# An f32 two-block transformer kernel on one core: the recurrent input's products dealt over the attention steps, the chunk copies of the start split over two engines, the table transposes behind the third product

## The chip, the cores and the metric

The kernel runs on 1 core of one Trainium2 chip. The metric is the device time of one execution in microseconds (us). The kernel before took 1950.97 us (median of 3 runs, 1947.81 to 1953.01).

The engines in the trace: PE is TensorE's matmul (PEld its weight load), DVE is VectorE, ACT is ScalarE, POOL is GpSimd, SP is SyncE, which here only issues DMAs. `acc` is the accumulator memory (PSUM): 4 places of 2 halves, each half 512 f32 numbers wide on 128 partitions, which is one bank.

## The reference, cut to what matters

512 tokens, with 16 meta tokens ahead in the first block, and a width of 1024. The first block has two layers: a norm, a wide projection, a pooling branch, latent attention with 8 heads, gates, and an output projection. The second block has one layer: a norm, a projection into q, k, v, the recurrent unit's input and gate, differential attention, the recurrent unit, and a mixture of experts. The change touches the start of the first block and this part of the second:

```python
q, k, v, lru_x, lru_g, gate_pre = jnp.split(proj, SPLIT_POINTS, axis=-1)
...
    def one_block(q_blk):                      # 4 query blocks of 128, 8 heads
        s = jnp.einsum('bqhcd,bkhcd->bhcqk', q_blk, k) * scale
        p = jax.nn.softmax(s, axis=-1)
        p_diff = p[:, :, 0] - lam * p[:, :, 1]
        return jnp.einsum('bhqk,bkhd->bqhd', p_diff, v)
...
xr = centred_depthwise_conv(lru_x, conv_w[l], conv_b[l])
h_fwd = rg_lru(xr, ...)                        # scan over the tokens, forwards
h_bwd = rg_lru(xr, ...)                        # and backwards
y_lru = (h_fwd + h_bwd) * jax.nn.gelu(lru_g)
```

## The kernel before, in words

All data lie with the model's width on the partitions, in 8 chunks of 128, and the tokens along the free side (528 with the meta tokens, 512 in the second block). Each product of f32 data is made from three passes, with an upper and a lower part of weights and data: upper weight by upper data, upper weight by lower data, lower weight by upper data. So a product of 1024 by 128 columns has 8 chunks x 3 = 24 passes over 512 tokens (`product3`, L1066 of the kernel before), or 48 over two halves of 264 (`product_split`, L834). The upper parts of weights are copied by ScalarE (L1449), the lower ones by VectorE (L2098), or by GpSimd for some (L2984).

The order of the work on each engine is the order of the code; engines wait for each other by semaphores. TensorE's results go to the four places of `acc` in turn: `accumulator` (L783) takes place `len(jobs) % 4` and first waits until the user of four jobs ago has been read. `drained` waits for all four.

The start: the input's four blocks of 128 tokens and the meta tokens come in as rows. For each chunk c TensorE turns four 128 x 128 blocks (L872) and the 16 meta columns (L873); VectorE copies both out (L2116, L2117); ScalarE makes the chunk's upper part (L1495), VectorE its lower part (L2110). Three weights' parts are made in between. Then follow the transposes of a vector table (`vec2`, L877) and of the rotary table (`trig`, L883), `drained`, and `first_products` (L851), which takes both its accumulators first and then goes chunk by chunk. ScalarE squares the chunks (L1444) and GpSimd adds the squares (L2898); the sum goes through `ss_h` behind the third product, and ScalarE's first evacuation (L1525, L1526) waits for it too.

The second attention has 32 items (8 heads x 4 query blocks) in 35 steps. In step s TensorE makes the scores of item s (`scores2`, L1138), an input product `lx` where `background2_at(s)` names one (8 products, one in every fourth or fifth step, the last in step 34), turns the probabilities of item s-2 (`turn2`, L1146), and multiplies the values of item s-3 (`values2`, L1155). VectorE takes the maximum (L2530) and its product with the scale (L2531), weighs the two softmaxes of item s-1 (`weigh`: L2519 to L2523), and copies `lx` out (L2537). ScalarE makes the exponentials (L1805), and copies out the turned probabilities (L1817) and the results (L1820). GpSimd makes the convolution of each `lx` chunk (L3000 to L3005) and the lower parts of `lx` weights 4 to 7. Behind the loop come the gate products `lg`, for whose weights 2 and later VectorE's lower parts stand behind the decay constants (L2544 to L2557).

## Time and profile before

| | |
|---|---|
| median of 3 runs | 1950.97 us |
| the profiled execution, its own time | 1950.18 us |
| its span, first to last instruction | 1948.2 us |
| TensorE busy | 1818.8 us, 93% |
| VectorE busy | 1176.4 us, 60% |
| ScalarE busy | 887.0 us, 46% |
| GpSimd busy | 332.0 us, 17% |
| mean granted TensorE clock | 0.978 |

A busy share is a mean over stages. The page's chain of the work that ended last has PE in 75% of the span and DVE in 15%. A number in square brackets in the timeline's rows is the idle time of the engine ahead of the row, with what ended it. The granted clock is a share of 2.4 GHz: 1.00 is that level, 0.50 the level of 1.2 GHz.

### The profile page before, as it was taken

The page shows a single profiled execution, that of the slowest core. Times are in us where ns is not written, and L with a number is a line of the kernel's source. Part 1 is how long each engine was busy: PE and PEld are TensorE (multiplying, and loading weights), DVE is VectorE, ACT ScalarE, POOL GpSimd, SP SyncE. Part 2 cuts the span into 40 slices and gives each one's busy share as a digit, 9 for nine tenths or more (in the row PEclk, how much of TensorE's full clock was granted, in tenths as well). Part 3 has the DMA queues.
Part 4 walks back from the last instruction along what each step waited for, and adds up shares of the span by engine and source line. Part 5 has one row for each costly group of instructions (what it writes and reads, how often), then busy time and mean ns, then how long its engine had stood idle before and what let it go on. Part 6 is the DMA issues. An engine that isn't in the chain of part 4 may idle for free.

```text
span 1948.2 us, 27574 instructions
## 1 busy us (share of the span) xinstructions
PE 1818.8 (93%) x11244; PEld 1542.0 (79%) x11244; DVE 1176.4 (60%) x1712; ACT 887.0 (46%) x1440; POOL 332.0 (17%) x223
## 2 busy tenths in 40 slices
PE   6999999999999999999999788899989979999993
PEld 5988788999998788999999556655568857777772
DVE  5565544554365544545774677586764456878786
ACT  3425434334334434334343454246652246777762
POOL 3332222001333222001000264510010000000001
PEclk9999999999999999999999899999999989999997
DMA  5202111223212211323222010112143258999994
GB/s 176 71 33 82 54 34 44 88 87 109 90 55 71 66 44 44 94 87 109 78 85 96 30 44 22 47 62 86 65 165 105 87 190 294 385 373 385 376 373 170
DMA packets 156103, 241.44 MB, mean 124 GB/s; under 512 B 9593, under 2 KB 101018, under 8 KB 155978
## 3 DMA queue, kind: packets, MB, share of 16 engines
q1 hardware_dynamic: 148602, 212.88, 32.4%
q0 software_dynamic: 4464, 16.25, 2.2%
q10 hardware_dynamic: 2912, 10.55, 1.3%
q8 instruction: 90, 1.47, 0.3%
q14 instruction: 35, 0.29, 0.1%
HBM read 223.41 MB, written 16.25 MB: 123 GB/s over the span
## 4 chain that ended last, share of the span: by engine, by line
PE 75%; DVE 15%; ACT 5%; issue 3%; DMA 1%; POOL 1%; SPq 0%; ACTq 0%; POOLq 0%; DVEq 0%
PE acc L834 31%; PE acc L1066 11%; PE acc L1290 9%; PE acc L1091 6%; PE acc L933 4%; PE acc L997 3%; DVE ring_split L2744 2%; PE acc L974 2%; DVE rt L2530 1%; PE acc L851 1%; PE acc L985 1%; DVE hres_split L2744 1%; PE acc L1276 1%; PE acc L1051 1%; PE acc L954 1%
## 5 line engine op out<-in xcount | busy, mean ns | idle before, releaser
L834 PE MATMUL acc<-h_split,ring_split 128*128 128x264 f32 x1088 | 309.7, 285 | 0.0
L834 PEld LDWEIGHTS acc<-h_split,ring_split 128*128 128x128 f32 x1088 | 205.7, 189 | 0.0
L834 PE MATMUL acc<-h_split,qk_split 128*128 128x264 f32 x384 | 109.7, 286 | 0.0
L834 PE MATMUL acc<-ring_split,qk_split 128*128 128x264 f32 x384 | 108.7, 283 | 0.0
L1091 PE MATMUL acc<-ring_split,h_split 128*128 128x256 f32 x384 | 107.9, 281 | 0.0
L1066 PE MATMUL acc<-h_split,ring_split 128*128 128x512 f32 x256 | 101.9, 398 | 0.0
L834 PE MATMUL acc<-h_split,krope_split 128*128 128x264 f32 x320 | 94.7, 296 | 3.9 <-ACT latent L1628 2.6
L834 PE MATMUL acc<-ring_split,krope_split 128*128 128x264 f32 x320 | 91.4, 286 | 0.0
L2098 DVE TENSOR_TENSOR ring_split<-ring,o_split 128x1024 fp32r<-128x1024 f32 (+1 forms) x32 | 44.8, 1415 | 74.8 <-ACT o_split L1449 74.8
L1290 PE MATMUL acc<-qk_split,krope_split 128*128 128x512 f32 x240 | 75.8, 397 | 8.8 <-DVE ring_split L2744 6.5
L3022 POOL DMA_INDIRECT latent<-h_rows,rows_of x16 | 18.3, 1145 | 382.9 <-PE acc L1276 230.0
L2098 DVE TENSOR_TENSOR ring_split<-ring,qk_split 128x1024 fp32r<-128x1024 f32 (+1 forms) x56 | 59.5, 1069 | 34.8 <-ACT qk_split L1449 34.6
L2898 POOL TENSOR_TENSOR latent<-latent 128x528 f32<-128x528 f32 x18 | 26.8, 1486 | 314.1 <-ACT latent L1444 313.8
L2912 POOL TENSOR_TENSOR ring_split<-ring,krope_split 128x1024 fp32r<-128x1024 f32 x20 | 48.1, 2407 | 168.7 <-ACT krope_split L1449 168.7
L997 PE MATMUL acc<-latent,v 128*64 128x128 f32 (+2 forms) x464 | 73.7, 283 | 0.9 <-ACT latent L1648 0.8
L834 PE MATMUL acc<-work_split,qk_split 128*128 128x264 f32 x256 | 72.9, 285 | 0.0
L834 PE MATMUL acc<-upad_split,ring_split 128*128 128x264 f32 x256 | 72.7, 284 | 0.0
L834 PEld LDWEIGHTS acc<-h_split,qk_split 128*128 128x128 f32 x384 | 72.3, 188 | 0.3 <-issue 0.3
L1091 PEld LDWEIGHTS acc<-ring_split,h_split 128*128 128x128 f32 x384 | 72.3, 188 | 0.0
L834 PEld LDWEIGHTS acc<-ring_split,qk_split 128*128 128x128 f32 x384 | 72.2, 188 | 0.0
L2744 DVE TENSOR_TENSOR ring_split<-ring,qk_split 128x2048 fp32r<-128x2048 f32 x24 | 54.0, 2292 | 27.5 <-ACT qk_split L1969 27.5
L1449 ACT ACTIVATE qk_split<-ring 128x1024 fp32r<-128x1024 f32 (+2 forms) x60 | 57.6, 967 | 25.7 <-PE acc L834 22.4
(572 smaller groups left out, 5806.9 us busy)
## 6 DMA issues: line engine op xcount, KB each, us to landing
ring<-in_w_in SPq DMA_DIRECT2D x64, 1024.0 KB, 5.3
ring<-in_w_expert_gate SPq DMA_DIRECT2D x13, 2048.0 KB, 9.8
ring<-in_w_expert_up SPq DMA_DIRECT2D x12, 2048.0 KB, 11.0
ring<-in_w_expert_down SPq DMA_DIRECT2D x11, 2048.0 KB, 12.1
ring<-in_w_out SPq DMA_DIRECT2D x12, 1024.0 KB, 5.7
hres<-in_w_expert_down SPq DMA_DIRECT2D x5, 2048.0 KB, 10.1
hres<-in_w_expert_up SPq DMA_DIRECT2D x4, 2048.0 KB, 11.3
y_rows<-gate ACTq DMA_DIRECT2D x16, 512.0 KB, 7.2
```

The source lines that it names most:

```text
L834: ins = nc.tensor.matmul(dst[0:rows_, half, 0:HALF], w[:, k, :], x[:, c], start=(k == 0 and i == 0), stop=(k == last and i == 2), skip_gro ...
L933: ins = nc.tensor.matmul(dst[0:nt, half, 0:width], x, w[:, c], start=(k == 0 and part == 0), stop=(k == count - 1 and part == 2), skip_gro ...
L974: ins = nc.tensor.matmul(dst[0:nt, c0:c1], qT[0:QK, hd, t0:t0 + nt], kT[0:QK, hd, c0:c1], start=True, stop=True)
L997: ins = nc.tensor.matmul(dst[r:r + VD, 0, 0:nt], v[0:nk, j, hd * VD:(hd + 1) * VD], probsT[s % 2][0:nk, j, 0:nt], start=(j == 0), stop=(j ...
L1066: ins = nc.tensor.matmul(dst[:, 0, :], w[:, k, :], x, start=(k == 0 and i == 0), stop=(k == DC - 1 and i == 2), skip_group_check=True)
L1091: ins = nc.tensor.matmul(dst[:, side, 0:WIDE], x[k][:, rows_], w, start=(k == 0 and part == 0), stop=(k == DC - 1 and part == 2), skip_gro ...
L1290: ins = nc.tensor.matmul(dst, x, w, start=start and i == 0, stop=stop and i == 2, skip_group_check=True)
L1449: nc.scalar.activation(dst, src, ACT.Copy).then_inc(act_made, 1)
L2098: made(nc.vector.tensor_tensor(dst, src, up.bitcast(F32), ALU.subtract), label)
L2744: nc.vector.tensor_tensor(granule_half(i, half, "low"), granule_half(i, half, "raw"), granule_half(i, half, "up").bitcast(F32), ALU.subtra ...
L2898: ins = nc.gpsimd.tensor_tensor(latent[:, 0, :] if c < DC - 1 else sum_sq, latent[:, 0, :], latent[:, c, :], ALU.add)
L2912: nc.gpsimd.tensor_tensor(dst, src, up.bitcast(F32), ALU.subtract).then_inc(pool_made, 1)
```

## The change

Three things.

**The input's passes are dealt over the steps.** A table says how many of the 8 x 24 = 192 passes each step makes: none in step 0, 24 in step 1, six in each of steps 2 to 25, two in each of 26 to 31, six in 32 and in 33, none in 34. `lx_passes` makes them behind the step's scores. The loop has its own places: scores alternate between places 0 and 1, a turning takes half 0 of place 2, `lx` half 1 of place 2, and values the halves of place 3 in turn. Each place is released by its own last reader. VectorE reads `lx` out ahead of `weigh`.

**The input chunks are copied by two engines.** ScalarE copies chunks 2, 5 and 7, VectorE the others. The meta tokens of all chunks are turned first into one place and copied at once.

**The tables' transposes** (`vec2`, `trig`) stand behind the third product and `ss_h` of layer 0; `drained` is gone from the start. VectorE's copies of them stand behind the reciprocal of `ss_h`.

```diff
+        LX_PASSES = 3 * DC
+        passes_at = [0, LX_PASSES] + [6] * 24 + [2] * 6 + [6, 6, 0]
+        passes_to = [sum(passes_at[:step]) for step in range(STEPS2 + 1)]
         def background2_at(step):
-            return range((step * DC) // STEPS2, ((step + 1) * DC) // STEPS2)
+            return range(passes_to[step] // LX_PASSES, passes_to[step + 1] // LX_PASSES)
...
             pe.wait_ge(x_loaded, 80)
+            dst = accumulator("meta", dve_evacuated)
             for c in range(DC):
-                dst = accumulator(("x", c), dve_evacuated)
+                ins = nc.tensor.transpose(dst[:, 0, c * META:(c + 1) * META], metain[0:META, c * P:(c + 1) * P],
+                                          ident[0:META, 0:META])
+            done(ins, "meta")
+            for c in range(DC):
+                dst = accumulator(("x", c), act_evacuated if c in X_BY_ACT else dve_evacuated)
                 for i in range(4):
-                    nc.tensor.transpose(dst[:, 0, i * P:(i + 1) * P], xin[:, i, c * P:(c + 1) * P], ident)
...
-            drained()
...
+                        if n.layer == 0:
+                            n.layer = None
+                            turn_tables()
+                            n.layer = 0
...
+            def place2_of(label, reader, slot, part):
+
+                for x in [users2[slot, part]] if (slot, part) in users2 else before2.get(slot, []):
+                    released(*x)
+                users2[slot, part] = (label, reader, n.layer)
+                n.slots[label, n.layer] = slot
+                return acc[:, slot, :, :]
+
+            def lx_passes(step):
+
+                for x in range(passes_to[step], passes_to[step + 1]):
+                    c, x = divmod(x, LX_PASSES)
+                    k, part = divmod(x, 3)
+                    label, i = ("lx", c), job_no2["lx", c]
+                    if x == 0:
+                        by = pool_made if i in LOW_BY_POOL else dve_made
+                        pe.wait_ge(by, at(by, ("wlow",) + label))
+                        lx_at.append(place2_of(label, dve_evacuated, 2, 1)[:, 1, :])
+                    w1, w0 = weight2_up(i), columns2(f"lx{c // 2}", c % 2, ring_split)
+                    w, moved = ((w1, h2_up), (w1, h2_low), (w0, h2_up))[part]
+                    ins = nc.tensor.matmul(lx_at[-1], w[:, k, :], moved[k], start=x == 0, stop=x == LX_PASSES - 1,
+                                           skip_group_check=True)
+                    if x == LX_PASSES - 1:
+                        done(ins, label)
...
-                dst = accumulator(("s2", s), act_evacuated)
+                dst = place2_of(("s2", s), act_evacuated, s % 2, 0)
...
-                dst = accumulator(("t2", s), act_evacuated)
+                dst = place2_of(("t2", s), act_evacuated, 2, 0)
...
-                dst = accumulator(("o2", s), act_evacuated)
+                dst = place2_of(("o2", s), act_evacuated, 3, s % 2)
...
-                for c in background2_at(s):
-                    product3(("lx", c), dve_evacuated, h2_up, h2_low)
+                lx_passes(s)
...
+                if c in X_BY_ACT:
+                    act.wait_ge(psum_filled, at(psum_filled, ("x", c)))
+                    nc.scalar.activation(hres[:, c, META:T], acc[:, n.slot(("x", c)), 0, :], ACT.Copy)\
+                        .then_inc(act_evacuated, 1)
...
-                if 1 <= s <= len(items2):
-                    weigh(s - 1)
                 for c in background2_at(s):
...
-                    evacuated(tt(lru_x[:, c, 1:1 + S], result2(("lx", c)), inv2, ALU.mult), ("lx", c))
+                    result2(("lx", c))
+                    evacuated(tt(lru_x[:, c, 1:1 + S], acc[:, 2, 1, :], inv2, ALU.mult), ("lx", c))
+                if 1 <= s <= len(items2):
+                    weigh(s - 1)
```

How the instructions stand now. TensorE in the second attention, from the last passes of an input product on; L1066 is a pass of the input product, L1146 a turning, L1155 the values, L1138 the scores. Before:

```order
L1066 MATMUL acc<-h_split,o_split 128x512
L1066 MATMUL acc<-ring_split,o_split 128x512
L1066 MATMUL acc<-h_split,ring_split 128x512
L1146 MATMUL acc<-const,v 128x128 x4
L1155 MATMUL acc<-upad,work 128x128 x4
L1138 MATMUL acc<-qk 128x512 x2
L1146 MATMUL acc<-const,gate 128x128 x4
L1155 MATMUL acc<-upad,work 128x128 x4
L1138 MATMUL acc<-qk 128x512 x2
L1146 MATMUL acc<-const,krope 128x128 x4
L1155 MATMUL acc<-upad,work 128x128 x4
L1138 MATMUL acc<-qk 128x512 x2
```

After, one step from turning to turning and the next (L1173 is a pass, L1195 a turning, L1204 the values, L1187 the scores):

```order
L1195 MATMUL acc<-const,gate 128x128 x4
L1187 MATMUL acc<-qk 128x512 x2
L1173 MATMUL acc<-h_split,o_split 128x512
L1173 MATMUL acc<-ring_split,o_split 128x512
L1173 MATMUL acc<-h_split,ring_split 128x512
L1173 MATMUL acc<-h_split,o_split 128x512
L1173 MATMUL acc<-ring_split,o_split 128x512
L1173 MATMUL acc<-h_split,ring_split 128x512
L1195 MATMUL acc<-const,krope 128x128 x4
L1204 MATMUL acc<-upad,work 128x128 x4
L1187 MATMUL acc<-qk 128x512 x2
```

The 24 passes that stood in one step stand as six behind each step's scores, ahead of the turning.

TensorE at the start, from the last chunk's transposes to the first passes of `first_products` (L851). Before:

```order
L872 MATMUL acc<-const,qk 128x128 x4
L873 MATMUL acc<-const,qk 128x16
L877 MATMUL acc<-const,qk 128x121
L883 MATMUL acc<-const,trig 16x32
L883 MATMUL acc<-const,trig 128x32 x4
L883 MATMUL acc<-const,trig 16x32
L883 MATMUL acc<-const,trig 128x32 x4
L851 MATMUL acc<-h_split,o_split 128x264
L851 MATMUL acc<-ring_split,o_split 128x264
L851 MATMUL acc<-h_split,ring_split 128x264
```

After: all meta columns (L879), all chunks (L885), and the first passes at once (L859).

```order
L874 MATMUL acc<-const,qk 128x44
L879 MATMUL acc<-const,qk 128x16 x8
L885 MATMUL acc<-const,qk 128x128 x32
L859 MATMUL acc<-h_split,o_split 128x264
L859 MATMUL acc<-ring_split,o_split 128x264
L859 MATMUL acc<-h_split,ring_split 128x264
```

And where the tables went: behind the third product (L842) and `ss_h` (L821), ahead of the fourth product.

```order
L842 MATMUL acc<-h_split,ring_split 128x264
L821 MATMUL acc<-gate,ones 128x264 x2
L891 MATMUL acc<-const,qk 128x121
L897 MATMUL acc<-const,trig 16x32
L897 MATMUL acc<-const,trig 128x32 x4
L897 MATMUL acc<-const,trig 16x32
L897 MATMUL acc<-const,trig 128x32 x4
L842 MATMUL acc<-h_split,o_split 128x264
L842 MATMUL acc<-ring_split,o_split 128x264
```

ScalarE at the start, behind the rotary table: L1495 makes a chunk's upper part, L1449 a weight's, L1444 the squares. Before:

```order
L1437 ACTIVATE trig<-krope,small 32x528
L1495 ACTIVATE h_split<-hres,vecs 128x528 x2
L1449 ACTIVATE o_split<-ring 128x1024
L1495 ACTIVATE h_split<-hres,vecs 128x528
L1449 ACTIVATE o_split<-ring 128x1024
L1495 ACTIVATE h_split<-hres,vecs 128x528 x3
L1449 ACTIVATE zp_split<-ring 128x1024
L1495 ACTIVATE h_split<-hres,vecs 128x528 x2
L1444 ACTIVATE latent<-hres 128x528 x8
```

After (L1546 a chunk's upper part, L1499 a weight's, L1555 the copy of a chunk out of `acc`):

```order
L1486 ACTIVATE trig<-krope,small 32x528
L1546 ACTIVATE h_split<-hres,vecs 128x528
L1499 ACTIVATE o_split<-ring 128x1024
L1546 ACTIVATE h_split<-hres,vecs 128x528
L1499 ACTIVATE o_split<-ring 128x1024
L1555 ACTIVATE hres<-acc 128x512
L1546 ACTIVATE h_split<-hres,vecs 128x528 x3
L1499 ACTIVATE zp_split<-ring 128x1024
L1555 ACTIVATE hres<-acc 128x512
L1546 ACTIVATE h_split<-hres,vecs 128x528 x2
L1555 ACTIVATE hres<-acc 128x512
L1546 ACTIVATE h_split<-hres,vecs 128x528
```

Three copies came in, and each of the three weights moved ahead by one chunk (behind chunks 0, 1 and 4 instead of 1, 2 and 5).

## Rows read from the trace of the kernel before

**Rows 1.** The page's first part: busy us, share of the span, instructions.

```profile
PE 1818.8 (93%) x11244; PEld 1542.0 (79%) x11244; DVE 1176.4 (60%) x1712; ACT 887.0 (46%) x1440; POOL 332.0 (17%) x223
```

**Rows 2.** Stretches: length, busy us of each engine, mean clock, DMA share, GB/s.

```profile
50.00:110.00 60.00, 60.00 (x490) 59.32 (x489) 37.03 (x34) 25.11 (x33) 24.57 (x11) 1.00 0.23 75
...
1079.41:1235.45 156.04, 131.49 (x705) 92.36 (x704) 108.24 (x211) 77.41 (x202) 74.91 (x53) 0.96 0.09 28
```

**Rows 3.** Timeline, TensorE, both ends of the loop: start, length, what, idle before.

```profile
1079.41 2.85 PE L1138 MATMUL acc<-qk 64*128 64x512 f32 x12
...
1089.92 1.11 PE L1146 MATMUL acc<-const,gate 128*128 128x128 f32 x4 [7.66 <-DVE gate L2523]
...
1234.40 1.05 PE L1155 MATMUL acc<-upad,work 128*128 128x128 f32 x8
```

**Rows 4.** Chain of waits, one block in the loop: start, length, what.

```profile
1114.57 5.85 PE acc L1066 x24
1120.42 0.44 PE acc L1146 x4
1120.85 0.89 PE acc L1155 x8
1121.75 1.08 PE acc L1138 x4
```

**Rows 5.** Chain of waits, VectorE's maxima, two pairs of neighbours.

```profile
1129.74 1.15 DVE rt L2530
...
1132.76 1.15 DVE rt L2530
...
1180.15 1.24 DVE rt L2530
...
1184.25 1.14 DVE rt L2530
```

**Rows 6.** Timeline of the loop: ScalarE's exponentials of step 1, VectorE's input.

```profile
1088.00 0.69 ACT L1805 ACTIVATE krope<-acc,rt 128x512 f32<-128x512 f32 x1
...
1217.32 0.69 DVE L2537 TENSOR_TENSOR latent<-acc,inv 128x512 f32<-128x512 f32 x1 [2.88 <-PE acc L1066]
```

**Rows 7.** Stretches, TensorE alone, then all engines; mean clock third from the end.

```profile
1086.00:1088.00 2.00, 0.00 (x0) 0.50 0.00 0
...
1115.00:1150.00 35.00, 31.56 (x176) 21.93 (x174) 24.77 (x49) 17.89 (x48) 19.57 (x14) 1.00 0.10 31
```

**Rows 8.** Timeline of the start, three engines.

```profile
11.16 1.12 PE L872 MATMUL acc<-const,qk 128*128 128x128 f32 x4
...
14.66 0.74 ACT L1495 ACTIVATE h_split<-hres,vecs 128x528 fp32r<-128x528 f32 x1 [0.53 <-DVE hres L2117]
...
15.31 1.04 ACT L1449 ACTIVATE o_split<-ring 128x1024 fp32r<-128x1024 f32 x1
...
15.43 0.68 DVE L2117 COPY hres<-acc 128x512 f32<-128x512 f32 x1
...
16.25 0.72 ACT L1495 ACTIVATE h_split<-hres,vecs 128x528 fp32r<-128x528 f32 x1
...
16.70 1.22 DVE L2098 TENSOR_TENSOR ring_split<-ring,o_split 128x1024 fp32r<-128x1024 f32 x1
...
22.60 1.12 PE L883 MATMUL acc<-const,trig 32*16 32x32 f32 x10 [0.90 <-DVE hres L2117]
...
28.72 0.59 PE L851 MATMUL acc<-h_split,o_split 128*128 128x264 f32 x1 [5.00 <-DVE trig L2140]
```

**Rows 9.** Chain of waits, projections of both layers.

```profile
28.72 14.02 PE acc L851 x96
...
49.45 34.81 PE acc L834 x288
...
490.15 11.64 PE acc L851 x96
```

**Rows 10.** Timeline, GpSimd's last addition of the squares.

```profile
36.66 1.34 POOL L2898 TENSOR_TENSOR gate<-latent 128x528 f32<-128x528 f32 x1
```

More of the change, by code:

```diff
@@ L786, in accumulator @@
                 if len(jobs) >= ACCS:
-                    released(*jobs[-ACCS])
-                jobs.append((label, reader, n.layer))
+                    for x in jobs[-ACCS]:
+                        released(*x)
+                jobs.append([(label, reader, n.layer)])
                 n.slots[label, n.layer] = slot
@@ L796, in drained @@
             def drained():
-                last = {x[1].name: x for x in jobs[-ACCS:]}
+                last = {x[1].name: x for users in jobs[-ACCS:] for x in users}
                 for x in last.values():
@@ L1167, in _ @@
                     values2(s - 3)
+            jobs[:] = [[x for (slot, part), x in users2.items() if slot == i] for i in range(ACCS)]
             for c in range(DC + LAG):
@@ L2120, in _ @@
+            evacuated(nc.vector.tensor_copy(hres[:, :, 0:META], src), "meta")
+            dve.wait_ge(dve_evacuated, at(dve_evacuated, "meta"))
+            for c in range(DC + 1):
+                if c < DC and c not in X_BY_ACT:
+                    result(("x", c))
+                    evacuated(nc.vector.tensor_copy(hres[:, c, META:T], acc[:, n.slot(("x", c)), 0, :]), ("x", c))
                 if c:
-                    dve.wait_ge(dve_evacuated, at(dve_evacuated, ("x", c - 1)))
+                    by = act_evacuated if c - 1 in X_BY_ACT else dve_evacuated
+                    dve.wait_ge(by, at(by, ("x", c - 1)))
@@ L2173, in _ @@
                 inverse("ss_h", inv[:, :])
+                if n.layer == 0:
+                    n.layer = None
+                    turned_tables()
+                    n.layer = 0
                 for i in range(6, DC):
```

105 lines of the change are left out of this document (56 added, 49 removed).

## The prediction

> **What bounds the kernel now.** I began with the page's busy shares: TensorE is busy 93% of the span [rows 1], so only places where it waits, or works at half clock, can give time back. Then I read the table of stretches. In the dense projections TensorE is busy in 60.00 of 60 us; in the loop of the second attention, from 1079.41 to 1235.45, it is busy 131.49 of 156.04 us, VectorE 108.24 and GpSimd 74.91, at a mean clock of 0.96 [rows 2]. So that loop waits, and no engine fills it. The timeline shows its two ends [rows 3]: the first scores at 1079.41, a wait of 7.66 us before the first turning of probabilities, and the last values ending at 1234.40 + 1.05 = 1235.45.
>
> The chain of waits shows the pattern inside [rows 4]. A whole input product of 24 passes runs 5.85 us as one block; behind it come a turning (0.43 to the next start), the values (0.90) and the next scores (1.08, with what follows 1.10), and only then VectorE's maximum. During the block VectorE and ScalarE run dry; after it TensorE waits for them, since a step without a block lasts what VectorE needs: 3.02 us from maximum to maximum, up to 4.10 with GpSimd working beside it [rows 5]. The two bounds are thus paid one after the other: about 124 us of TensorE work (below) stand in 156.
>
> The second place is the start. The first products begin at 28.72, after a wait of 5.00 us for VectorE's copies of the turned tables, while the chunks' own parts were ready long before [rows 8].
>
> **The loop, part by part.** Nothing is taken from or added to the matrix work: 192 passes, 32 scores, turnings and values. What changes is the order and the places. Before, every user took the next of four places in turn; now scores alternate between two, a turning and the input product each have a half of the third, and values alternate in the halves of the fourth. So an input product can stay open over four steps without holding up anyone, and its release falls to VectorE's one multiplication, 0.69 us [rows 6].
>
> One pass costs 5.85 / 24 = 0.24 us; a group of six 1.46, and I add 0.06 for starting each group behind another kind of product (an estimate: the block's last pass lasts longer than its share too). A six-pass step of TensorE is then 1.52 + 0.43 + 0.90 + 1.10 = 3.95 us [rows 4]. VectorE needs 3.02 free of GpSimd, at the worst 4.10 [rows 5], and 0.69 / 4 = 0.17 for its share of the input's multiplication. GpSimd's convolution is busy about half of the loop [rows 2], so VectorE's mean is near 3.5 + 0.17 = 3.7: under 3.95, by little. The order in the step leaves room: turning s is issued two steps after its scores, 7.9 + 2.6 = 10.5 us after their start, while maximum, exponentials, the next maximum and the weighing are done after some 8.5 us. That slack of 2 us covers a single step of 4.10 + 0.69.
>
> The sum, by TensorE's clock on the wall. Scores 0 and 1 begin at 1079.41 and end at 1081.4. The whole first product follows, 24 passes, until 1087.2: it fills the wait of 7.66 us. Scores 2 need the exponentials of step 0, which end at 1088.0, where those of step 1 begin [rows 6]; their VectorE inputs don't change. Scores, six passes and the first turning bring step 3 to 1091.1. Steps 3 to 25 are 23 x 3.95 = 90.9, to 1182.0. Steps 26 to 31 carry two passes each, so there VectorE sets the pace again: 6 x 3.3 = 19.8, less 1.5 of slack used up, to 1200.3. Step 32 (six passes, turning, values) 2.85 and step 33 the same, to 1206.0, the last values 0.9 more, 1206.9. For single waits on VectorE and ScalarE (an upper part of the next weights, 1.04 us [rows 8], now also lies in such a step) I add 1.5: 1208.4. The loop ends 1235.45 - 1208.4 = 27.0 us earlier. Bounds: with no such wait and no group start 30; with VectorE pacing every six-pass step at 4.27 it is 27.0 - 23 x 0.32 = 19.7.
>
> Behind the loop stand, for VectorE, two lower parts of weights and the decay constants. In both kernels they are released by the last input product, the last turning and the last values, in this order, so they move with the loop's end; the last product now ends a step earlier, which is worth nothing there, because the second lower part waits for the last turning. The loads of the later weights hang on products that now end earlier still.
>
> **The start, part by part.** The sixteen meta columns get one place and one VectorE copy: 7 small copies and 8 single turnings between chunks go, 8 small turnings stand ahead of chunk 0. From ten small ones in 1.12 us [rows 8] I take 0.9, so chunk 0 is turned at 12.05 to 13.15 instead of 11.16 to 12.3. Three of eight chunk copies (0.68 each on VectorE [rows 8]) go to ScalarE, where I take 0.65. The tables' eleven transposes leave the place where TensorE emptied all accumulators, and stand behind the third product and its sum. That is what takes the wait of 5.00 away; what is late next is chunk 5. The second accumulator of the first products is the one that chunk 5 had, and chunk 5 is now ScalarE's to copy. ScalarE's line up to it, at the pitches of before (0.65 for a chunk operation, 0.94 for a weight [rows 8]): chunk 0 in memory at 13.9, upper 0, weight 0, upper 1, weight 1 to 17.1. VectorE (a weight's lower part 1.2, the rest 0.7): lower weight 0 to 16.9, lower 1, lower weight 1 to 18.8, copy 3, lower 2, copy 4 to 20.8. ScalarE again, waiting for copy 4: upper 4, weight 2, copy 5, to 23.1. So the first products start at 23.2 instead of 28.72. They still run at the lower pace first: here 96 took 14.02, and the same 96 in the second layer, warm, 11.64 [rows 9]. 23.2 + 14.0 = 37.2; the third product 5.8 (34.81 / 6), the sum of squares 0.9 (49.45 - 42.74 - 5.80), the tables 0.9: the fourth product starts at 44.8 instead of 49.45, 4.6 us earlier. The sum of squares needs GpSimd's last addition, which ended at 38.0 [rows 10], and ScalarE's list ends about when it did, so it is in time; the fourth product now also needs the third's evacuation (43.0, and two copies of about 0.5 on ScalarE: 44.0), also in time. Bounds: 6 if ScalarE is quicker; 1.5 if chunk 5 waits longer or TensorE, fed by chunks, takes longer to reach its full pace. From there to 110 TensorE is always busy [rows 2], so the gain goes on to the end.
>
> GpSimd's and SyncE's lists keep their order; the loads move with the products that free their places.
>
> **Sum.** The profiled execution took 1950.18, its span 1948.2. 1950.18 - 27.0 - 4.6 = 1918.6. It stood 0.8 under the median of 1950.97, so I forecast 1919.
>
> **Rivals.** (A) VectorE paces the loop. For it: the step from 1180.15 to 1184.25 took 4.10 with GpSimd working [rows 5], and GpSimd's 75 us now lie in a loop of 129 us instead of 156. If all six-pass steps cost 4.27, the loop gains 19.7: 1926. Against it: most steps beside GpSimd lie well under 4.10. The Trainium skill's SBUF — State Buffer, Who interferes with whom, says that a VectorE instruction with two SBUF inputs blocks fully against a GpSimd one that reads SBUF; by that rule denser convolutions make the weighing wait for whole GpSimd instructions, which speaks for this rival; the trace agrees that such steps are longer.
>
> (B) Something behind a gain takes it back: the products behind the start wait for ScalarE's parts, or those behind the loop for VectorE's decay constants. Half of the start's gain and 4 us at the loop's end would go: 1925. TensorE is full behind the start [rows 2], which speaks against the first.
>
> (C) Slower: the clock falls inside the loop. Idle TensorE fell to 0.50 in the wait at the loop's start, and stood at 1.00 from 1115 to 1150, where its waits are short [rows 7]. If the new steps, cut into four small groups with waits between, let it fall, each us of warm work costs one more. The gain of 31.6 is used up when 31.6 / 3.95 = 8 of the 23 six-pass steps run at half clock; with 12 the time is 1919 + 47 = 1966. Against it: waits between groups get shorter, not longer. The Trainium skill's TensorE: Matmul & The Clock Gate, A second HAM failure mode: psum-queue depth-cycling, describes such an oscillation for a kernel that cycled through banks each iteration; that is this rival's mechanism, and the trace does not bear it out, with 1.00 in steps that cycled through four places.
>
> (D) The dealt passes gain nothing, because some reader still holds the input's place or the turning waits for it: 1950.97 - 4.6 = 1946. Order and places speak against it.
>
> **How the numbers follow.** Forecast 0.72, its own range 1914 to 1923; A 0.12, B 0.09, C 0.03, D 0.02, and 0.02 for slower by a cause I don't see. The range from 1912 to 1932 takes in the forecast, A and B and the bounds (loop 19.7 to 30, start 1.5 to 6, so 1950 - 36 = 1914 to 1950 - 21 = 1929), with 3 us for what no row shows. Faster by over 0.3% (6 us, about what can be told from no change) takes in the forecast, A, B and part of D: 0.94; within 0.3% 0.02; slower 0.04.
>
> **What would show it.** After: the loop's stretch about 129 us with TensorE busy over 95% of it at clock 1.00; scores to scores 3.9 to 4.0 in steps 3 to 25, and no wait of 1 us before a turning there; no wait of 7.66; the first products starting near 23.2, with the fourth near 44.8. Steps of 4.2 or more, ended by VectorE, would show A; a clock of 0.50 in the loop, C. The forecast is wrong in its main step if TensorE waits for turnings inside six-pass steps.

## The result, and the profile after

The changed kernel took 1921.35 us (median of 4 runs, 1920.62 to 1922.58) against 1949.39 of the kernel before (4 runs, 1945.62 to 1953.01): a ratio of 0.9845, 95% interval 0.983 to 0.986. The ratios given here and below are not the quotients of the two medians (here 0.9856); they differ from these by up to 0.002. The forecast was 1919.0 with a range of 1912 to 1932, so the time came out faster and inside. The profiled execution took 1922.02 with a span of 1920.2; the span of before was 1948.2, so the two traces are 28.0 us apart, and that is what has to be found in them.

The page first: busy us, share of the span, instructions, to be put beside [rows 1].

```profile
span 1920.2 us, 27569 instructions
PE 1813.5 (94%) x11244; PEld 1538.0 (80%) x11244; DVE 1179.7 (61%) x1702; ACT 887.8 (46%) x1443; POOL 331.0 (17%) x223
```

Then the stretches: after the projections the loop, from its first scores to its last values, and a part of it. Columns as in [rows 2].

```profile
1071.10:1203.31 132.21, 128.50 (x706) 88.48 (x706) 114.54 (x211) 76.43 (x202) 76.23 (x54) 1.00 0.11 35
1115.00:1150.00 35.00, 35.00 (x196) 24.43 (x195) 31.64 (x56) 19.88 (x55) 27.70 (x21) 1.00 0.10 31
```

The loop takes 132.21 us instead of 156.04 [rows 2]. TensorE's work in it is nearly the same, 128.50 busy (131.49 before, at a lower mean clock), but the idle time in it fell from 24.5 to 3.7 us, and from 1115 to 1150 there is none (before, 31.56 of 35 busy [rows 7]). VectorE's own busy time grew from 108.24 to 114.54 with the same 211 instructions.

The chain of waits of after gives the milestones at the start and behind it.

```profile
22.94 13.74 PE acc L859 x96
44.15 35.00 PE acc L842 x288
341.47 140.39 PE acc L842 x1152
1117.30 1.59 PE acc L1173 x6
1121.28 1.60 PE acc L1173 x6
1218.50 18.43 PE acc L1084 x72
1415.02 113.63 PE acc L1084 x480
```

The first products start at 22.94 (28.72 before [rows 8]), the fourth product at 44.15 (49.45 [rows 9]). Two groups of six passes in a row start 3.98 apart, where before a block of 24 ran 5.85 [rows 4]. The table follows the lead of after over before at the same piece of work. Its entries for before come from that kernel's chain of waits, except the loop's, which are [rows 3].

| piece of work | before | after | lead | gained in between |
|---|---|---|---|---|
| fourth product starts | 49.45 | 44.15 | 5.3 | start: 5.3 |
| dense products of layer 0 start (x1152) | 349.76 | 341.47 | 8.3 | first attention: 3.0 |
| loop starts | 1079.41 | 1071.10 | 8.3 | 0 |
| loop ends | 1235.45 | 1203.31 | 32.1 | loop: 23.8 |
| last long product starts (x480) | 1447.92 | 1415.02 | 32.9 | 0.8 |
| that product ends | 1559.38 | 1528.65 | 30.7 | -2.2 |
| span's end | 1948.2 | 1920.2 | 28.0 | -2.7 |

So the two changed places give 29.1, and three stretches in which nothing was changed move by 3.0, -2.2 and -2.7; with the 0.8 behind the loop that makes 28.0.

What waits are left in the loop is told by the waits by releaser, TensorE, 1071 to 1204 (waited for: us in total, times, longest).

```profile
PE acc L1195 <- ACT upad L1877: 1.7, 2, 1.2
PE acc L1195 <- DVE krope L2588: 1.1, 1, 1.1
PE acc L1187 <- ACT gate L1865: 0.9, 1, 0.9
```

These three lines hold all 3.7 us of idle time: one wait for the first exponentials, one before the turning of step 3 (the second turning of all), and two for ScalarE near the loop's end. The wait of 7.66 before the first turning [rows 3] is gone.

### The profile page after: what moved, and what is told of

It reads as the page before. It is cut to its first block, busy times and chain, and to the rows that moved or that the text cites. A ratio compares the mean times of both kernels' runs of the same rounds, so it can differ in the third digit from the quotient of the medians.

```text
span 1920.2 us, 27569 instructions
## 1 busy us (share of the span) xinstructions
PE 1813.5 (94%) x11244; PEld 1538.0 (80%) x11244; DVE 1179.7 (61%) x1702; ACT 887.8 (46%) x1443; POOL 331.0 (17%) x223
## 4 chain that ended last, share of the span: by engine, by line
PE 78%; DVE 13%; ACT 5%; issue 2%; DMA 1%; POOL 1%; SPq 0%; ACTq 0%; POOLq 0%; DVEq 0%
PE acc L842 31%; PE acc L1339 10%; PE acc L1084 8%; PE acc L1109 7%; PE acc L951 4%; PE acc L1015 3%; DVE ring_split L2810 2%; PE acc L992 2%; PE acc L1173 2%; PE acc L1187 1%; PE acc L1204 1%; PE acc L859 1%; PE acc L1003 1%; DVE hres_split L2810 1%; DVE v L2510 1%
## 5 line engine op out<-in xcount | busy, mean ns | idle before, releaser
L842 PE MATMUL acc<-h_split,ring_split 128*128 128x264 f32 x1088 | 308.4, 283 | 0.0
L842 PEld LDWEIGHTS acc<-h_split,ring_split 128*128 128x128 f32 x1088 | 204.3, 188 | 0.0
L842 PE MATMUL acc<-h_split,qk_split 128*128 128x264 f32 x384 | 109.7, 286 | 0.0
L842 PE MATMUL acc<-ring_split,qk_split 128*128 128x264 f32 x384 | 108.7, 283 | 0.0
L842 PE MATMUL acc<-h_split,krope_split 128*128 128x264 f32 x320 | 94.0, 294 | 3.8 <-ACT latent L1688 2.4
L842 PE MATMUL acc<-ring_split,krope_split 128*128 128x264 f32 x320 | 90.8, 284 | 0.0
L1084 PE MATMUL acc<-h_split,ring_split 128*128 128x512 f32 x192 | 77.4, 403 | 0.0
L842 PE MATMUL acc<-work_split,qk_split 128*128 128x264 f32 x256 | 72.9, 285 | 0.0
L842 PE MATMUL acc<-upad_split,ring_split 128*128 128x264 f32 x256 | 72.7, 284 | 0.0
L842 PEld LDWEIGHTS acc<-h_split,qk_split 128*128 128x128 f32 x384 | 72.3, 188 | 0.3 <-issue 0.3
L842 PEld LDWEIGHTS acc<-ring_split,qk_split 128*128 128x128 f32 x384 | 72.2, 188 | 0.0
L1499 ACT ACTIVATE qk_split<-ring 128x1024 fp32r<-128x1024 f32 (+2 forms) x60 | 57.7, 967 | 25.6 <-PE acc L842 24.0
## 6 DMA issues: line engine op xcount, KB each, us to landing
hres<-in_w_expert_up SPq DMA_DIRECT2D x4, 2048.0 KB, 10.8
```

Source lines behind the costliest of these rows:

```text
L842: ins = nc.tensor.matmul(dst[0:rows_, half, 0:HALF], w[:, k, :], x[:, c], start=(k == 0 and i == 0), stop=(k == last and i == 2), skip_gro ...
L1084: ins = nc.tensor.matmul(dst[:, 0, :], w[:, k, :], x, start=(k == 0 and i == 0), stop=(k == DC - 1 and i == 2), skip_group_check=True)
L1499: nc.scalar.activation(dst, src, ACT.Copy).then_inc(act_made, 1)
```

## The experiments

All times stand beside runs of the kernel before on the same chip: 1950.21 in the first four, 1952.6 in the next four, 1950.62 in the last four. "Loop" is the stretch from the first scores to the last values in each profiled execution.

### The two parts alone

e1 has the old start and the new loop; e2 the new start and the old loop, with its four places in turn.

```
e1: start as before;  passes_at = [0, 24] + [6] * 24 + [2] * 6 + [6, 6, 0], own places in the loop
e2: start as after;   24 passes where background2_at(s) names a product, places in turn
```

> The loop's part alone, on the start of before (chunks copied by VectorE, tables turned ahead of the first products, accumulators emptied). Theory: the two parts add up. The loop lasts 132 us as in the changed kernel (156 before), the first products start at 28.7 and the fourth product at 49.5, so the time is 1949.4 - 23.8 = 1925.6, give or take what the clock does elsewhere (1923 to 1929). Rival: the loop's gain needs the earlier start (the weights of the loop come in time only so): the loop over 140, time over 1933. A second rival on the 3.2 us that the first attention gained beside: if that came from the clock's phase and not from the change, its stretch from the fourth product of before (49.45) to the dense projections (349.76) keeps its 300.3 here, or takes any other value within some 3 us, though nothing before it changed.

> The start's part alone, with the loop of before. Theory: first products at 22.9, fourth product at 44.2, loop 156, time 1949.4 - 5.1 = 1944.3, and up to 3.2 less if the first attention repeats the clock of the changed kernel (297.3 us from the fourth product to the dense projections). Rival: the start's lead is lost again in the token units or the attention of the first layer, where TensorE waits for VectorE: then the dense projections start less than 3 us earlier than 349.8 and the time is 1947 or more.

e1: 1928.29 us, ratio 0.9885 (0.9866 to 0.9904); loop from 1079.65 to 1211.79, 132.1 us. e2: 1947.13, ratio 0.9995 (0.9974 to 1.0015); fourth product at 44.16, dense products at 341.55, loop from 1071.18 to 1226.23, 155.05 us. The loop's gain is there alone and whole. The start's lead is there too, 8.2 us at the dense products, but only 3.9 us of it reach the span's end (1944.3), and by the times of e2 it can't be told from nothing. So the time is the rival's (1947 or more), but not by the rival's cause, which asked for a lead under 3 us at the dense products. Set beside e1, the start does show: e1's ratio of 0.9885 and the changed kernel's 0.9845 have intervals that don't touch.

### Dealing or places

e3 keeps the own places and deals nothing. Its blocks stand in steps 1, 5, 9 to 29, those of before in steps 4, 8, 13 to 34:

```
-        passes_at = [0, LX_PASSES] + [6] * 24 + [2] * 6 + [6, 6, 0]
+        passes_at = [0] + [LX_PASSES, 0, 0, 0] * 8 + [0, 0]
```

> The changed kernel with each input product's 24 passes in one step again (steps 1, 5, 9 to 29), but with the accumulator places of the change. Theory: the dealing makes the gain, since VectorE and ScalarE run dry behind a whole block and TensorE waits for VectorE in the steps between; the loop lasts 146 to 152 us (8 blocks of 5.85, 32 steps of 3.1 to 3.5, the wait at the loop's start filled), time 1921.4 + 14 to 20 = 1935 to 1941. Rival: the own places make the gain (turnings, values and scores no longer queue behind the product's reader): the loop lasts 132 to 138 us, time 1921 to 1927.

1944.46 us, ratio 0.9975 (0.9961 to 0.9989). Its loop takes 162.0 us, 6 more than before, and its stretch (columns as in [rows 2]) and TensorE's waits in it are these.

```profile
1071.33:1233.29 161.96, 132.16 (x706) 91.86 (x706) 123.19 (x211) 77.63 (x202) 86.77 (x60) 0.97 0.10 33
```

```profile
PE acc L1195 <- ACT upad L1877: 10.7, 9, 2.6
PE acc L1195 <- DVE krope L2588: 6.5, 4, 3.1
PE acc L1195 <- DVE v L2588: 5.9, 4, 2.0
PE acc L1195 <- DVE gate L2588: 5.8, 5, 2.0
```

Both theories had the loop too short (146 to 152, and 132 to 138). All of the loop's gain needs the dealing; own places without it gain nothing. Dealing with the places in turn wasn't tried, so how much of the gain needs the own places is not shown. Why this loop is even longer than the one before isn't separated either: there are more waits for ScalarE, the blocks stand in other steps, with none in the last five, and GpSimd is busy 86.77 instead of 74.91 us, with 60 instructions instead of 53 in the loop, since the last block is done earlier.

e9 deals half as finely, twelve passes in every second step:

```
+        passes_at = [0, LX_PASSES] + [12, 0] * 12 + [2] * 6 + [6, 6, 0]
```

> The sixes of steps 2 to 25 are dealt as twelve passes in every second step and none between; everything else is the changed kernel's. Whole blocks of 24 in every fourth step took a loop of 162.0 us, sixes 132.2. Theory (a turning stands two steps behind its scores, so VectorE and ScalarE have two steps' worth of TensorE's time for it; what counts is that any two steps in a row hold twelve passes, not that each holds six): the loop takes 132 to 135 and the time is 1921 to 1924. Rival (a step without passes lasts 2.5 us on TensorE and VectorE needs 3.0 to 3.5, so each of twelve such steps waits 0.5 to 1 us or more): the loop takes 138 to 144 and the time is 1927 to 1933.

1937.64 us, ratio 0.9932 (0.991 to 0.9953); loop from 1081.95 to 1226.15, 144.2 us, TensorE busy in 130.98 of it. The rival was right on the loop, and my idea that two steps' sum is enough was wrong. Its time is above the rival's 1927 to 1933. Its seven executions run from 1930.05 to 1945.44, and in the profiled one, which took 1945.03, the loop starts 10.8 us later than in the changed kernel, by the clock in the first attention (below).

e5 deals all products evenly, which sets edges of products inside groups:

```
+        passes_at = [0, LX_PASSES] + [6, 5, 5, 5] * 8 + [0]
```

> Passes dealt evenly: 24 in step 1, then 6, 5, 5, 5 in turn to step 33, instead of sixes until step 25, twos in steps 26 to 31 and sixes in 32 and 33. In the changed kernel's trace steps 26 to 31 took 19.6 us with two passes each, while TensorE's own work in them is some 18. Theory (TensorE sets the pace of every step that has five or six passes, and the short steps at the end are where VectorE and ScalarE show): 32 steps of 5.25 passes on average cost 3.985 - 0.75 x 0.24 = 3.80 each; the loop takes 130.5 to 131.5 us instead of 132.2, the waits of 0.55 and 1.19 for ScalarE's probabilities go or shrink, and the time is 1919.5 to 1921. Rival (VectorE sets the pace nearly everywhere, at 3.9 and more): five-pass steps take as long as six-pass steps, the loop becomes 133 to 135, the time 1922 to 1924.

1928.21 us, ratio 0.9876 (0.986 to 0.9893); loop 141.5 us. Longer than either theory gave, and by something neither had. The timeline of TensorE at the first such edge, and of VectorE beside it:

```profile
1098.01 0.39 PE L1173 MATMUL acc<-h_split,ring_split 128*128 128x512 f32 x1
1099.72 0.47 PE L1173 MATMUL acc<-h_split,zp_split 128*128 128x512 f32 x1 [1.32 <-DVE latent L2601]
```

```profile
1098.89 0.69 DVE L2601 TENSOR_TENSOR latent<-acc,inv 128x512 f32<-128x512 f32 x1
```

The next product's first pass stands right behind the last one of the product before, in the same half of a place, and waits until VectorE has read it out: 7.1 us in five waits. In sixes the edges of products fall on edges of steps, and a turning, values and scores (2.4 us) lie between. Of the 9.3 us that this loop is longer, 7.1 are these waits, and 2.6 are TensorE's longer busy time (131.10 instead of 128.50) at a mean clock of 0.99.

### The order on VectorE

e4 weighs item s-1 before it reads the input product out:

```
-   for c in background2_at(s): ... read lx out ...
-   if 1 <= s <= len(items2): weigh(s - 1)
+   if 1 <= s <= len(items2): weigh(s - 1)
+   for c in background2_at(s): ... read lx out ...
```

> The changed kernel with VectorE's weighing ahead of its read of the finished input product, as before. Theory: the order is worth little, since in six-pass steps TensorE waits for neither: the read ends about 5.0 us behind the step's scores, the next product's first pass is due at 5.05; loop 132 to 133.5, time 1921 to 1923. Rival: the read in front of the weighing is what costs the waits for turnings (1.07 in step 3, and in step 26), and with the weighing first the loop gets 1 us shorter or more.

1923.32 us, ratio 0.9861 (0.9842 to 0.988); loop 135.2 us, 3.0 longer, with a wait of 1.3 for the product's place and waits of 0.9 and 0.6 before turnings. In time it can't be told from the changed kernel. The order is worth more than I expected (132 to 133.5), and the rival had its sign wrong. The changed order is the better one by 3 us in the traces; the x480 product took 111.47 here and 113.63 there, which hides most of it.

### The 3.2 us that the loop fell short

e6 moves GpSimd's lower part of a weight behind the convolution of its step; e10 deals the last product in threes.

```
e6:  weights2_lower(job_no2["lx", 4 + c]) behind the convolution of chunk c
e10: passes_at = [0, LX_PASSES] + [6] * 24 + [3] * 8 + [0]
```

> GpSimd makes its four lower weight parts of the input product behind the convolution of the same step instead of ahead of it. Theory (the first turning wait of 1.07 us in the loop comes from a VectorE instruction of 128x2 that took 1.56 us beside GpSimd's 2.35 us lower part): that instruction takes 0.17 again or another one is stretched by less, the turning of step 3 starts without a wait, the loop takes 131.0 to 131.4 instead of 132.2, the time is 1920.0 to 1920.6. Rival (GpSimd's work stretches VectorE wherever it lies, as the convolution is no kinder than the lower part): the wait moves to a neighbouring step and the time stays at 1921 to 1922; a loop longer than 132.5 would mean that the late lower part now holds up a product.

> The last product's 24 passes are dealt as three in each of steps 26 to 33, instead of two in 26 to 31 and six in 32 and 33; group edges still fall on product edges. Theory (steps 26 to 31 last 3.27 us on average because VectorE and ScalarE pace them, and TensorE's own work with three passes is 3.985 - 0.73 = 3.26): these steps keep their length, steps 32 and 33 have 1.4 us less, of which the wait for ScalarE in step 32 takes back about half; the loop takes 131.3 to 131.8 instead of 132.2, the time is 1920.5 to 1921. Rival (TensorE's time adds up even there): the loop keeps 132.2 or gets longer, up to 133, and the time is 1921 to 1922. The loop's length in the trace tells, the time can't.

In the changed kernel a VectorE instruction on 128x2 numbers takes 1.56 us, 0.17 elsewhere, while GpSimd makes a lower part:

```profile
1082.17 2.35 POOL L3050 TENSOR_TENSOR ring_split<-ring,o_split 128x1024 fp32r<-128x1024 f32 x1 [153.57 <-ACT o_split L1499]
...
1082.99 1.56 DVE L2596 TENSOR_SCALAR rt<-rt 128x2 f32<-128x2 f32 x1
...
1086.73 0.63 PE L1195 MATMUL acc<-const,krope 128*128 128x128 f32 x4 [1.07 <-DVE krope L2588]
```

In e6 (1925.09 us, 1918.75 to 1929.42, ratio 0.9853, 0.9829 to 0.9876) the loop takes 132.3 us. The wait before that turning went from 1.07 to 0.52, for ScalarE, and a small instruction two steps later was stretched instead:

```profile
1101.41 2.36 POOL L3050 TENSOR_TENSOR ring_split<-ring,o_split 128x1024 fp32r<-128x1024 f32 x1
...
1101.48 2.31 DVE L2596 TENSOR_SCALAR rt<-rt 128x2 f32<-128x2 f32 x1
```

So the cause is shown, since it moved with GpSimd's instruction, and moving it is worth nothing: the rival. The time lies above what either gave, by a first attention 10 us longer (below).

In e10 (1921.81 us, 1918.41 to 1923.69, ratio 0.9847, 0.9833 to 0.9862) the loop takes 132.0. The short steps that follow one another without a wait last 3.28 us with three passes and 3.05 to 3.17 with two; the one step of 3.8, with a wait for ScalarE, is in both. Steps 32 and 33 are shorter, and step 32 waits 1.66 for ScalarE instead of 1.19. Even with two or three passes a step is thus mostly TensorE's own time, and VectorE doesn't pace it. The rival was nearer.

### The start

e12 gives all chunk copies back to VectorE:

```
-        X_BY_ACT = (2, 5, 7)
+        X_BY_ACT = ()
```

> All eight copies of the input chunks are VectorE's again, with the meta columns' single copy and the tables' transposes as in the changed kernel. Theory (the copies dealt to ScalarE take 3 x 0.68 us off VectorE's line, which the first products wait for last): the first products start 1.5 to 2.5 us later than at 22.94, at 24.5 to 25.5, the fourth product at 45.7 to 46.7, and the time is 1922 to 1924 with the clock's differences behind on top. Rival (the moved transposes alone make the start's gain, since ScalarE's line was as long as VectorE's): the first products start within 0.5 us of 22.94.

1919.90 us, ratio 0.9845 (0.9831 to 0.986). The first products start here:

```profile
22.29 0.56 PE L859 MATMUL acc<-h_split,o_split 128*128 128x264 f32 x1 [2.06 <-DVE hres L2181]
```

That is 0.65 earlier than in the changed kernel, against my theory of 1.5 to 2.5 later. Half of it is the load's: TensorE's first instruction waits for it, and it came at another time in each trace (10.34 to 11.58). First the changed kernel, then e12:

```profile
10.67 0.30 PE L874 MATMUL acc<-const,qk 44*128 44x44 f32 x1 [10.67 <-DMA qk<-in_k_norm_gain]
```

```profile
10.34 0.30 PE L874 MATMUL acc<-const,qk 44*128 44x44 f32 x1 [10.34 <-DMA qk<-in_k_norm_gain]
```

From that instruction to the first products it is 12.27 or 12.28 us in the eleven traces that have three copies on ScalarE, 11.95 in e12, and 17.79 and 17.80 in before and e1. So the copies on ScalarE cost 0.32 there, and the fourth product starts at 44.20 against 44.15. Dealing the copies over two engines is worth nothing; the start's gain must come from what e12 keeps, the moved transposes of the tables without `drained` and the single copy of the meta columns, which were not tried apart.

### Behind the loop

In the changed kernel TensorE waits 4.04 us behind the loop, for a lower part that stands behind the decay constants on VectorE:

```profile
1205.75 1.27 DVE L2610 TENSOR_SCALAR decay<-vec 128x16 f32<-128x16 f32 x1
...
1213.19 1.22 DVE L2619 TENSOR_TENSOR decay<-decay 128x16 f32<-128x16 f32 x1
1214.44 0.17 DVE L2620 TENSOR_SCALAR decay<-decay 128x16 f32<-128x16 f32 x1
...
1217.13 1.22 DVE L2159 TENSOR_TENSOR ring_split<-ring,trig_split 128x1024 fp32r<-128x1024 f32 x1
...
1218.50 0.77 PE L1084 MATMUL acc<-h_split,trig_split 128*128 128x512 f32 x1 [4.04 <-DVE ring_split L2159]
```

e7 moves them ahead of the loop, e11 is e7 with the threes of e10:

```
-            for i in range(2 * DC + 4, 2 * DC + 12):
+            for i in range(2 * DC + 4, 2 * DC + 10):
                 weights2_lower(i)
+            (lambda and the decay constants)
+            for i in range(2 * DC + 10, 2 * DC + 12):
+                weights2_lower(i)
```

> VectorE's lambda and its decay constants (22 small operations that took 11.3 us behind the loop, five of them 1.2 us long instead of 0.17) stand ahead of the last two lower parts before the loop, where VectorE waits 9 us for ScalarE; ScalarE's two exponentials for them move along. Theory (behind the loop TensorE waits 4.04 us for the lower part of a weight that stands behind these constants): that wait goes, the stretch from the last values to the 72-pass product shrinks from 15.2 to about 11.2, and the time is 1917 to 1918. Rival (the next things are late too, ScalarE's parts or the loads, or the later stages give it back): under 1.5 us is gained, 1920 to 1922.

> The changed kernel with the constants ahead of the loop and the last product dealt in threes: the two together. Theory (the wait of 4.04 us behind the loop goes, as it did alone, the loop's end is 0 to 0.7 us shorter, and the loop's start may lose up to 2 us where VectorE's weighing falls beside GpSimd's lower part): the time is 1915 to 1919, below both the changed kernel and the constants alone or equal to the latter. Rival (the gain of the constants alone, which came out between 1913 and 1924 in single executions, was the clock's): 1920 to 1923.

e7 took 1916.74 us (1913.29 to 1924.47, ratio 0.9834, 0.9809 to 0.9859), e11 1916.72 (6 runs, 1912.58 to 1929.62, ratio 0.9839, 0.9817 to 0.9861). In e7 the constants take from 1065.77 to 1071.06, 5.3 us instead of 11.3, in a gap of VectorE; no operation of theirs is stretched. The wait of 4.04 is gone from both traces, and from the loop's end to the x480 product it is 205.9 and 206.0 us instead of 211.7. In e7 these 5.8 us are the wait of 4.04, one of 0.7 further on that is gone too, and 1.1 less busy time. The loop pays some of it back: a weighing beside GpSimd's lower part took 2.94 us instead of 0.75, and the first turning waits:

```profile
1080.99 2.94 DVE L2611 SCALAR_TENSOR_TENSOR gate<-gate,rt 128x512 f32<-128x512 f32 x1
...
1083.99 0.66 PE L1195 MATMUL acc<-const,gate 128*128 128x128 f32 x4 [2.01 <-DVE gate L2611]
```

Its loop takes 133.7, e11's 133.5. The net is 4.3 us in the trace of e7. The medians are 4.6 under the changed kernel's, but the ratios to the kernel before, 0.9834 and 0.9839 against 0.9845, lie inside each other's intervals, so the times don't show that either beats it.

### The stretches that nobody changed

e8 makes the tables' transposes behind the third product four times over, which should only shift the rest.

```
-   for j, x in enumerate((cosT, sinT)): ... transpose ...
+   for _ in range(4): for j, x in enumerate((cosT, sinT)): ... transpose ...
```

> The turning of the rotation tables behind the third product is done four times over instead of once (same result each time): 33 small turnings more on TensorE, 1.5 to 2.5 us, with nothing else changed. It shifts everything behind it by that much. Theory (what a later stage costs depends on where its waits fall against the clock's rises and falls, since the change's start made the first attention 3.2 us shorter and two later places together 4.9 longer with the same waits): stretches behind the shift change by more than 0.5 us against the changed kernel, in the first attention (until the dense products at 341.5) or at the wait of 3.8 us at 1406 to 1420, and the end is not simply 1.5 to 2.5 us later: anything from 1918 to 1927. Rival (these differences are the work's own): every stretch keeps its length within 0.3 us, and the time is 1923 to 1924.

1924.29 us, ratio 0.9862 (0.9846 to 0.9879). The fourth product starts at 46.29, 2.1 later than after, the dense products at 346.56, 5.1 later, and the x480 product takes 111.47 instead of 113.63. So the stretches don't keep their lengths, as the theory had it, but that the shift is the cause isn't shown. The shift isn't clean: 0.9 of the 2.1 is the load's, which came at 11.58, the first products took 13.30 instead of 13.74, and the transposes make the other 1.7. And executions of one and the same kernel differ as much without any shift (e9's by 15 us, e2's from 1943.8 to 1958.66). The first attention, from the fourth product's start to the dense products' (the same instructions in all kernels), took:

| length, us | in (fourth product's start) |
|---|---|
| 297.3 to 297.4 | after (44.15), e2 (44.16), e3 (44.33), e7 (44.38), e11 (43.96) |
| 298.7 to 298.9 | e4 (44.77), e5 (44.48), e10 (44.99), e12 (44.20) |
| 300.3 to 300.6 | before and e1 (49.45), e8 (46.29) |
| 307.5 to 307.6 | e6 (43.95), e9 (43.64) |

One thing goes with these lengths that the fourth product's start doesn't. The first products (x96) are where TensorE comes to its upper level: in the changed kernel the clock is 0.50 from 24 to 26 us and 1.00 from 28 on, and how long they took tells when it rose. Among the eleven kernels that have the start of the change and not e8's longer transposes, those in the first row took 13.65 to 13.75 us for them, those in the second 13.95 to 14.47, and e6 and e9 13.30 and 13.23. With the start of before (14.02, 14.34) and in e8 (13.30) the length is 300.3 to 300.6. Why an earlier or later rise there should go with 1.4 or 10 us more some 150 us behind it, no run here shows.

The stretch from 190 to 210 of after, of e8 and of e6, and the one from 210 to 230 of e6:

```profile
190.00:210.00 20.00, 18.28 (x98) 12.44 (x96) 13.70 (x40) 10.98 (x38) 5.17 (x4) 0.91 0.15 50
```

```profile
190.00:210.00 20.00, 18.28 (x104) 12.89 (x102) 12.13 (x34) 9.84 (x32) 3.99 (x4) 0.91 0.18 53
```

```profile
190.00:210.00 20.00, 18.28 (x83) 12.36 (x82) 11.64 (x34) 10.16 (x35) 5.16 (x4) 0.76 0.15 50
210.00:230.00 20.00, 19.74 (x90) 14.89 (x89) 6.67 (x22) 4.88 (x17) 1.29 (x1) 0.64 0.18 53
```

TensorE is busy as long in each, but e6 gets 83 matmuls done where after gets 98, at a mean clock of 0.76 (e8 also fell to 0.91 from 170 to 190, where after stood at 1.00). The second such place lies around the wait of 3.80 us ahead of the x480 product. Behind that wait, 10 us of the same work in after and in e4:

```profile
1411.00:1421.00 10.00, 8.49 (x23) 6.22 (x23) 5.17 (x7) 4.24 (x5) 3.96 (x7) 0.56 0.84 327
```

```profile
1414.86:1424.86 10.00, 8.49 (x32) 6.31 (x32) 5.23 (x8) 4.24 (x5) 3.97 (x7) 0.87 0.85 328
```

The same waits come before both. After them TensorE is at 0.56 in the mean in one and 0.87 in the other, 23 matmuls against 32, and that is the 2.2 us. The product took 113.6 to 113.7 us in four of the fourteen traces (after, e2, e3, e9) and 111.5 in the other ten. The third is the router, first 30 us of before, then the same work of after:

```profile
1590.73:1620.73 30.00, 18.94 (x94) 16.70 (x95) 19.81 (x25) 16.46 (x12) 5.96 (x4) 0.66 0.60 204
```

```profile
1560.00:1590.00 30.00, 19.26 (x76) 17.17 (x77) 19.00 (x24) 14.59 (x10) 5.26 (x3) 0.55 0.55 192
```

TensorE is busy for 19 us of both, at 0.66 and at 0.55. From the x480 product's end to the span's end it is 391.5 to 391.8 us in four traces (after, e2, e5, e9) and 388.4 to 389.2 in the other ten. So the changed kernel's trace has the longer value in both places, and before's the shorter one.

## Why the prediction was right

**The loop's mechanism: right.** Dealt passes fill the time that VectorE and ScalarE need (e1, e3, e9). The six-pass step was forecast at 3.95 and measured at 3.98 to 3.99; TensorE is busy in 97% of the loop at a clock of 1.00, and no wait for a turning comes in steps 4 to 25. Step 3 is the exception: its turning waits 1.07 us for VectorE, and the step takes 5.25. The prediction had named just that (a wait of 1 us before a turning in steps 3 to 25, a step over 4.2 ended by VectorE) as a sign of being wrong; it came once in 23 steps.

**Its size: 27.0 forecast, 23.8 measured.** Three terms were mis-sized. The first steps took 1.5 more (the scores of step 4 stand 17.1 us behind the loop's start, not 15.6), 1.07 of it the wait for the stretched small instruction. The six-pass steps cost 0.04 more, 0.8 over the 22 from step 4 on, since I gave 0.06 for starting a group, and six passes took 1.59 instead of 1.52. Steps 26 to 31 took 19.6 to the end of their last values, not 18.3: I let VectorE pace them and took 1.5 off for slack, while TensorE's own work alone is 3.05 in a two-pass step (3.17 and 3.32 where the turning starts 0.1 to 0.2 later), and one wait of 0.55 for ScalarE is added. The tail, with the 1.5 set aside for single waits, took 0.4 less than forecast: the waits there (1.19) were smaller than the reserve.

**The start: 4.6 forecast, 5.3 measured.** The first products came at 22.94 against 23.2, and took 13.74 against 14.0; 0.26 of the 5.3 is the load, which came at 10.67 instead of 10.93. The working was wrong where it let the copies on ScalarE help: e12 shows that they cost 0.32 instead of giving anything, so that 4.6 was near is in part luck. That the gain "goes on to the end" held by milestones up to the loop, but in e2's trace 3.9 of 8.2 arrive at the end, by the two stretches with the clock at its lower level for longer.

**Behind the loop: right that nothing is given or taken.** It is 0.8 from the loop's end to the x480 product. The wait of 4.04 for the constants' successor stayed, as in before (3.4 and 1.1), and moved along.

**The clock elsewhere: not in the sum.** 3.0 gained in the first attention, 2.2 and 2.7 lost behind, -1.9 together; the other traces show such amounts come and go with no change in the work, and that they nearly cancel here is luck. The sum's miss is the loop's -3.2, the start's +0.7, +0.8 behind the loop and -1.9: 3.6 us of the span, 28.0 instead of 31.6. By the executions' own times it is 3.4, 1918.6 against 1922.02.

**The rivals.** A (VectorE paces the loop): no, six-pass steps are 3.98 to 3.99, step 3 apart, although single instructions beside GpSimd are stretched, up to 2.94 us for a weighing in e7. The Trainium skill's SBUF — State Buffer, Who interferes with whom, which the prediction had put beside this rival, tells of such blocking for a VectorE instruction with two SBUF inputs. The trace agrees for single instructions (that weighing, 2.94 instead of 0.75), and the two steps between scores and turning absorb nearly all of it. B (something behind takes it back): a part, by the clock and not by ScalarE or VectorE. C (the clock falls in the dealt loop): no, 1.00; it is with blocks that it is lower (e3, 0.97, before 0.96). D: no.

## What to carry to other kernels

When an engine's long block alternates with a chain on other engines, deal the block over all steps and not over every second one, and let the edges of its products fall where other work lies between, or the single accumulator becomes the wait. Put small constants where their engine idles anyway, away from GpSimd's long instructions. Traces of kernels with the same work differed here by 2 to 10 us in stretches that nobody changed, so read a gain per stretch and not by the end alone. And before comparing two starts, take off the time at which TensorE's first load came.

## What the runs showed of the hardware

- A VectorE instruction beside a GpSimd one can last until that one ends, whatever its own size: 128x2 numbers took 1.56 and 2.31 us instead of 0.17 and ended at 1084.55 and 1103.79, 0.02 to 0.03 behind a lower part of 2.35. The constants' 128x16 operations took up to 1.3 us instead of 0.17 behind the loop, beside GpSimd's convolution and what follows it, and were not stretched in e7, where GpSimd did nothing beside them. It doesn't meet every instruction: most of the 128x16 ones beside GpSimd took 0.17 there too.
- The granted clock after the same waits isn't the same from one trace to the next. The first attention came in four lengths, 297.4, 298.8, 300.4 and 307.5 us, 10 us apart at the ends, for the same instructions, and the x480 product and all that follows it in two lengths each. What sets which of them a trace gets is open: the fourth product's start alone doesn't, since 43.95 gave 307.6 and 43.96 gave 297.3, while the moment at which the clock rose in the first products goes with it.
- The load that TensorE's first instruction waits for came 10.34 to 11.58 us behind the span's start in the fourteen traces, and with the changed start and three copies on ScalarE the first products followed 12.27 or 12.28 us behind it in all eleven.
